# Layer 0 of a two-layer backbone: context tiles first, and their expert rows beside the latent tiles' attention

## The reference, cut to what matters

```
tokens: 256 context (2 tiles of 128) and 512 latent (4 tiles of 128), D = 1024, two layers, float32
for each layer:
    h  = modulated RMSNorm(x);  p = h @ w_in                 # 3104 columns
    y  = concat(GLA scan, 2-D neighbourhood attention ("nat"),
                differential attention with axial rotary ("diff"))
    x += gate * (y @ w_out)
    h2 = modulated RMSNorm(x)
    q  = h2 @ wq;  16 best of 128 x 128 product keys in each of 8 heads  -> 128 experts a token
    x += gate * sum over the 128 of  softmax_weight * gelu(h2 . U[expert]) * V[expert]
# context tokens read context tokens only; the last layer updates latent tokens only
out = RMSNorm(x)                                             # latent tokens
```

## Time and profile before

| | us |
|---|---|
| median of 3 executions | 4746.25 |
| lowest, highest | 4745.8, 4751.58 |
| span of the profiled execution | 4741.8 |

### The profile page before, as it was taken

One profiled execution on the slowest core, in us unless ns is written; L12 is line 12 of the kernel. 1 busy time (PEld: TensorE's weight loads), 2 busy tenths in 40 slices (PEclk: granted clock), 3 DMA queues, 4 the chain that ended last, 5 costly groups with the idle time before them and its releaser, 6 DMA issues. The chain is left out here.

```text
span 4741.8 us, 35603 instructions
## 1 busy us (share of the span) xinstructions
PE 2298.1 (48%) x11329; PEld 1110.8 (23%) x11329; DVE 2751.2 (58%) x6329; ACT 543.2 (11%) x1141; POOL 2607.1 (55%) x2676
## 2 busy tenths in 40 slices
PE   7995778815025034052067286688904205115025
PEld 3433655401001010010015253365601001001001
DVE  2117756983873963954944800575895493683840
ACT  1005652100000000000000000354100000000000
POOL 1101300577777767767766663140377777777775
PEclk9997999958558567576568698799957658657556
DMA  6840002799999999999999998002499999999998
GB/s 226 269 159 18 20 2 105 290 409 409 409 409 409 409 405 405 409 400 409 409 397 403 404 403 323 28 21 76 176 391 409 410 409 409 409 405 406 410 408 338
DMA packets 451030, 1495.96 MB, mean 315 GB/s; under 512 B 59506, under 2 KB 91974, under 8 KB 444190
## 3 DMA queue, kind: packets, MB, share of 16 engines
q0 software_dynamic: 368640, 1342.34, 71.4%
q1 hardware_dynamic: 46056, 76.70, 4.7%
q10 hardware_dynamic: 36150, 74.65, 4.6%
HBM read 1477.38 MB, written 16.14 MB: 315 GB/s over the span
## 5 line engine op out<-in xcount | busy, mean ns | idle before, releaser
L1612 POOL DMA_INDIRECT experts_U<-in_peer_u_dram,experts_expert x768 | 729.3, 950 | 695.5 <-PE experts_acc L1831 425.4
L2158 DVE CUSTOM_DVE_ANT_0 experts_V<-experts_V,experts_acc 128x1024 f32<-128x1024 f32 x512 | 622.2, 1221 | 584.4 <-DMA experts_V<-in_peer_u_dram,experts_expert 565.1
L2158 DVE CUSTOM_DVE_ANT_0 experts_U<-experts_U,experts_acc 128x1024 f32<-128x1024 f32 x768 | 930.5, 1220 | 52.0 <-DMA experts_U<-in_peer_u_dram,experts_expert 24.0
L1619 POOL DMA_INDIRECT experts_V<-in_peer_v_dram,experts_turned x640 | 608.6, 951 | 266.5 <-issue 179.3
L1619 POOL DMA_INDIRECT experts_U<-in_peer_v_dram,experts_turned x640 | 608.3, 951 | 229.2 <-issue 172.1
L1974 PE MATMUL experts_pair<-small,experts_w 128*128 128x128 f32 x10 | 4.7, 475 | 1437.7 <-DVE experts_w L2117 1437.7
L1988 PE MATMUL experts_acc<-experts_U,experts_lent 128*32 128x512 f32 x2560 | 443.5, 826 | 346.3 <-DMA experts_U<-in_peer_v_dram,experts_turned 346.3
L1988 PE MATMUL experts_acc<-experts_V,experts_lent 128*32 128x512 f32 x2560 | 432.8, 808 | 327.0 <-DMA experts_V<-in_peer_v_dram,experts_turned 327.0
L1612 POOL DMA_INDIRECT experts_V<-in_peer_u_dram,experts_expert x512 | 485.7, 949 | 174.7 <-issue 106.8
L1974 PEld LDWEIGHTS experts_pair<-small,experts_w 128*128 128x128 f32 x10 | 1.8, 182 | 1440.2 <-DVE experts_w L2117 1440.2
L430 PE MATMUL proj_acc<-W,HT 128*128 128x512 f32 (+2 forms) x832 | 327.3, 548 | 3.9 <-DMA W<-in_w_in_dram 2.5
(11 more groups left out here) (286 smaller groups left out, 3534.6 us busy)
## 6 DMA issues: line engine op xcount, KB each, us to landing
proj_ada<-in_ada_w_dram ACTq DMA_DIRECT2D x40, 1024.0 KB, 5.8
W<-in_w_in_dram SPq DMA_DIRECT2D x9, 2048.0 KB, 11.7
experts_U<-in_peer_u_dram,experts_expert POOLq DMA_INDIRECT x768, 14.2
experts_QT<-in_w_in_dram ACTq DMA_DIRECT2D x12, 960.0 KB, 19.4
experts_V<-in_peer_v_dram,experts_turned POOLq DMA_INDIRECT x640, 12.7
experts_U<-in_peer_v_dram,experts_turned POOLq DMA_INDIRECT x640, 12.7
PR<-in_ada_w_dram SPq DMA_DIRECT2D x8, 1024.0 KB, 17.0
experts_U<-in_w_out_dram SPq DMA_DIRECT2D x4, 2048.0 KB, 11.7
```

What stands on the lines that cost most here:

```text
L1612: pool.indirect_dma_start(into, None, u_rows, bass.IndirectOffsetOnAxis(ap=s.expert[:, j % 2, k:k + 1], axis=0)).then_inc(done, 16)
L1619: pool.indirect_dma_start(into, None, v_rows, bass.IndirectOffsetOnAxis(ap=s.turned[:, j % 2, e:e + 1], axis=0)).then_inc(done, 16)
L2158: nc.vector.tensor_tensor_reduce(out=rows, in0=rows, in1=h_bank(), scale=1.0, scalar=0.0, op0=ALU.mult, op1=ALU.add, accum_out=s.dots[:, j ...
```

## The change

Layer 0's attention now runs for the two context tiles only (`near`), and a new function, `experts_first`, does everything after it. It writes the row work of all six tiles as one stream for each engine: a generator that says before each piece which row it belongs to. `Advance.upto(n)` issues the pieces of rows below n. The stream is issued in five stretches:

- `early_head`: output projection, norm, queries and experts of the context tiles; rows 0 to 63
- `attention` "nat" of the latent tiles in a `Window` of rows 64 to 171: after each of 22 steps (6 preparations and 16 units) every engine issues the stream up to `at(i)`
- `attention` "diff" of the latent tiles in the same manner: rows 172 to 287, 22 steps
- `late_head`, head of the latent tiles: rows 288 to 399, 13 steps (5 for tiles, 8 for query heads)
- the main stretch: rows 400 to 1535

Tiles go in the order 0 to 5, 256 rows each, so tile 0 is rows 0 to 255 and tile 1 rows 256 to 511. Rows below 512 use 8 buffers, later ones 16. The context tiles' dots read h from SBUF (`Y`), the latent ones from PSUM as before. In the windows the scores have one PSUM buffer (`S_BUFS`), and queries, keys and values are read back from DRAM: `gla_scores` stores them there (`mix`, 6 DMAs, 7.1 MB), since the projection's SBUF is given up. The rotary operations move from "nat" to `gla_gates` in both layers. Five tiles (AHEAD) instead of four are projected for layer 1, in 65 units, 6 beside tile 4's V rows, 36 beside tile 5's U rows and 23 beside its V rows; the fifth of them, tile 4, is normalised among tile 5's dots. Layer 1 projects one tile, tile 5, with all its columns, and loads five.

```
-HIDDEN = 4
+AHEAD = 5
...
                 if not first:
-                    for t in range(t1, NT):
-                        act.dma_start(PR[:, t], m.pr[(t - t1) * P:(t - t1 + 1) * P]).then_inc(kept, 16)
-                    act.wait_ge(kept, 16 * HIDDEN)
+                    for t in range(AHEAD):
+                        act.dma_start(PR[:, t], m.pr[t * P:(t + 1) * P]).then_inc(kept, 16)
+                    act.wait_ge(kept, 16 * AHEAD)
...
-            neighbourhood(nc, m, l, PR, Y)
-            if stop == "nat":
-                return
-            differential(nc, m, l, PR, Y)
+            near = list(range(CT)) if l == 0 else list(range(CT, NT))
+            attention(nc, m, l, PR, Y, "nat", near, gated=True)
+            attention(nc, m, l, PR, Y, "diff", near)
...
-        experts(nc, m, l, t0, Y, out)
+        if l == 0:
+            experts_first(nc, m, Y)
+        else:
+            experts(nc, m, l, t0, Y, out)
...
+        rope = Y[:, 0, 0:LT * P].rearrange("p (t c) -> p t c", c=P)
+        r1, r2 = Y[:, 1, 0:512], Y[:, 2, 0:512]
+        rotary, turned = st.sem("rotary"), st.sem("turned")
...
+                if l == 0:
+                    for t in range(NT):
+                        sp.dma_start(m.mix[t * P:(t + 1) * P], PR[:, t, NQ:PROJ]).then_inc(spilled, 16)
+                    sp.wait_ge(spilled, 16 * NT)
...
+    def upto(self, n):
+        while self.place is not None and self.place < n:
+            self.place = next(self.steps, None)
...
+    def at(self, i):
+        return self.first + (self.last - self.first) * (i + 1) // self.steps
+
+    def pool(self):
+        self.stream.pool.upto(self.last + RING)
...
-    first_wide = wide.index(1)
-    with Stage(nc, f"{kind}{l}") as st:
...
+    first_wide = wide.index(1) if any(wide) else 0
+    own_rows = window is not None
+    S_BUFS = 1 if own_rows else 2
...
+        F = st.ps("F", [P, 4 + 2 * S_BUFS, 512])
...
+                if own_rows and not diff:
+                    sp.dma_start(rows[:], m.mix[:, 0:768].rearrange("(t p) c -> p t c", p=P)).then_inc(vals_in, 16)
+                if own_rows and diff:
+                    for t in range(NT):
+                        if t:
+                            sp.wait_ge(prep, t)
+                        sp.dma_start(raw[:], m.mix[t * P:(t + 1) * P, DQ - NQ:DQ - NQ + 1024]).then_inc(raw_in, 16)
+                    sp.dma_start(vals[:], m.mix[:, DV - NQ:DV - NQ + 512].rearrange("(t p) c -> p t c", p=P)).then_inc(vals_in, 16)
...
+                    if window is not None:
+                        window.pe(t)
...
+                    if window is not None:
+                        window.pe(NK_T + u)
...
+                    if window is not None:
+                        window.dve(NK_T + u)
...
+    SMALL_RING = CT * ROWS
+    HEAD_END, NAT_END, DIFF_END, LATE_END = 64, 172, 288, 400
...
+            if n < SMALL_RING:
+                return s.U[:, n % RING], ug[n % RING], 16 * (n // RING + 1)
+            turn, p = (n - SMALL_RING) // PLACES, (n - SMALL_RING) % PLACES
...
+                yield ROWS * j + SLOTS
+                pe.wait_ge(weights, j + 1)
+                pe.wait_ge(turned, j + 1)
...
+                for g in range(GROUPS):
+                    steps = LATE_STEP_AT if j == 1 else STEP_AT
+                    if 0 < j < T - 1 and g in steps:
+                        yield ROWS * j + SLOTS + GROUP * g
+                        key_scores(nc, pe, s, sems, 4 * (j + 1) + steps.index(g), s.QT[:, j + 1 - CT])
+                    yield ROWS * j + SLOTS + GROUP * g + GROUP - 1
...
+                    weighted_sum(j, g)
...
+                    if k == 0 and j >= CT:
+                        dve.wait_ge(held_h, j - CT + 1)
+                    nc.vector.tensor_tensor_reduce(out=rows, in0=rows, in1=s.h_bank if j >= CT else Y[:, j],
+                                                   scale=1.0, scalar=0.0, op0=ALU.mult, op1=ALU.add,
+                                                   accum_out=s.dots[:, j % 2, k:k + 1]).then_inc(dots, 1)
+                    if k in (OUT_AT, OUT_AT + 2):
+                        next(adding, None)
+                    elif k == TURNED_AT[j]:
+                        dve.wait_ge(etr, j + 1)
+                        nc.vector.tensor_copy(s.turned[:, j % 2], tr[:, 0:P]).then_inc(turned, 1)
+                    elif j == 0:
+                        next(s.finding, None)
...
+                    for x in range(2):
+                        nc.vector.scalar_tensor_tensor(out=s.next_sc[x], in0=s.next_sc[x], scalar=1.0, in1=s.next_g,
+                                                       op0=ALU.add, op1=ALU.mult).then_inc(next_coef, 1)
+                    for i in range(3):
+                        next_average(i)
...
+                        if i == 2:
+                            next_average(3)
+                        next_norm(i)
+            for _ in add_out(T - 1):
+                pass
...
+        stream.pool, stream.pe = Advance(row_steps(nc.gpsimd)), Advance(product_steps(nc.tensor))
+        stream.act, stream.dve = Advance(scalar_steps(nc.scalar)), Advance(dot_steps(nc.vector))
+        early_head(nc, m, Y, s, sems, stream, HEAD_END, acc, link, spare, gain, stat, sub_rows, zeroed, gates)
+        attention(nc, m, l, None, Y, "nat", LAT, window=Window(stream, HEAD_END, NAT_END))
+        attention(nc, m, l, None, Y, "diff", LAT, window=Window(stream, NAT_END, DIFF_END))
+        s.V = st.sb("V", [P, RING, D])
+        late_HT, s.QT = st.sb("HT", [P, KD, LT * P]), st.sb("QT", [P, LT, PH, P])
+        late_head(nc, m, Y, s, Window(stream, DIFF_END, LATE_END), link, late_HT, spare, gain, stat, late_gates)
...
+            def _(pool):
+                pool.wait_ge(prods, 2 * T)
+                stream.pool.upto(end + RING)
...
+                evacuate("h", 1)
+                for _ in range(40):
+                    next(s.finding)
+                stream.dve.upto(end)
...
+                for i in range(T + 1):
+                    if i < T:
+                        norm_heads(i)
+                        evacuate("y", i)
+                        residual(i, 0)
+                        residual(i, 1)
+                        dve.wait_ge(squared, i + 1)
+                        nc.vector.tensor_scalar(stat[:, 1, i:i + 1], stat[:, 0, i:i + 1], 1.0 / D, EPS, ALU.mult, ALU.add).then_inc(mean, 1)
+                    if i:
+                        evacuate("h", i - 1)
+                    if i < T:
+                        dve.wait_ge(root, i + 1)
+                        link(nc.vector.reciprocal(stat[:, 1, i:i + 1], stat[:, 2, i:i + 1]))
+                        link(nc.vector.scalar_tensor_tensor(out=Y[:, t0 + i], in0=m.X[:, t0 + i], scalar=stat[:, 1, i:i + 1], in1=sc,
+                                                            op0=ALU.mult, op1=ALU.mult))
+                        nc.vector.tensor_tensor(Y[:, t0 + i], Y[:, t0 + i], sh, ALU.add).then_inc(hs, 1)
+                    window.dve(i)
+                for h in range(PH):
+                    window.dve(T + 1 + h)
...
-    tiles = list(range(NT - HIDDEN, NT)) + list(range(CT, NT - HIDDEN)) + list(range(t0, CT))
+    tiles = list(range(t0, NT))
...
```

More of the change, by code:

```diff
@@ L393, in project @@
     WR, BANKS, AR = PROJ_RING, 3, 2
-    t1 = NT - HIDDEN if last else NT
-    EARLY = min(t1 - 1, BANKS)
+    tiles = list(range(AHEAD, NT)) if last else list(range(NT))
+    EARLY = min(len(tiles) - 1, BANKS)
     TABLES_AT = [[], [], [0, 1], [2, 3], [4, 5], [6], [7]]
@@ L410, in project @@
             table_in, table_out, windowed = (st.sem(x) for x in ("tablein", "tableout", "windowed"))
-        chunks = [x for x in PROJ_CHUNKS if x[2] or not last or t1 > CT]
-        work = [(c, t) for c in range(len(chunks)) for t in range(t1) if chunks[c][2] or not last or t >= CT]
+        chunks = PROJ_CHUNKS
+        work = [(c, t) for c in range(len(chunks)) for t in tiles]
         kept = st.sem("kept")
@@ L436, in early @@
                     product(pe, i - 1)
[L438 removed]
+            norm_modulate(nc, m, l, m.a["norm1_g"][l], 0, tiles[0], NT, HT, st, block, ht, scratch, after=early, ready=first)
             def window_table(sp, n):
@@ L940, in _, with __init__, spread, pe @@
                 evacuate(len(tiles) - 1)
-def neighbourhood(nc, m, l, PR, Y):
-    attention(nc, m, l, PR, Y, "nat")
-def differential(nc, m, l, PR, Y):
-    attention(nc, m, l, PR, Y, "diff")
-def attention(nc, m, l, PR, Y, kind):
+class Advance:
+    def __init__(self, steps):
+        self.steps = steps
+        self.place = next(steps)
+    def upto(self, n):
+        while self.place is not None and self.place < n:
+            self.place = next(self.steps, None)
+class Window:
+    def __init__(self, stream, first, last):
+        self.stream, self.first, self.last = stream, first, last
+    def spread(self, steps):
+        self.steps = steps
+    def at(self, i):
+        return self.first + (self.last - self.first) * (i + 1) // self.steps
```

(41 more changed lines are left out.)

1062 lines of the change are left out of this document (819 added, 243 removed).

## The result

The changed kernel took 4983.89 us in the median of 4 executions (4982.18 to 4990.04), against 4748.91 for the kernel before beside it: a ratio of 1.050, interval 1.0485 to 1.0515, slower by 235 us. The profiled execution's span is 4988.0 us, 246.2 more than before. The forecast was 4888.

What follows compares the result with a forecast made beforehand. Stages bound by PE and DVE alternate with stages bound by DMA. 4746.25 us, plus 144 from "nat" to row 512, less 2 elsewhere, gave 4888; own range 4810 to 4970, whole range 4640 to 5010.

Steps and rivals of the forecast that it cites:

- Context attention and `early_head`: Layer 0's context attention alone, 65 us, then `early_head` with rows 0 to 63 and retrieval on DVE, 205 us.
- "nat" window: Latent "nat" attention beside rows 64 to 171: 186 us for 108 rows, V groups at 7.0 us each.
- "diff" window: Latent "diff" attention beside rows 172 to 287: 246 us; units 10.5 us beside V rows, 13.1 beside U rows.
- `late_head`: Latent tiles' head beside rows 288 to 399: 255 us, PE and DVE alternating at 34.2 us a step.
- rival 2: Context U rows: each context dot holds up a gather by 0.60 us; +55 us, 4943 us; chance 0.06.
- Eight buffers as the limit of V rows: Rows below 512: only two V groups under way, 7.0 us a group; rows 400 to 511 take 182 us.
- rival 4: V rows below 512: eight buffers suffice at 5.1 us a group; -107 us, 4781 us; chance 0.10.
- Rotary operations: Gates' stage of both layers: they slow DVE where both read SBUF, +5 us (0 to 20).
- The fifth tile: Main stretch: 13 more projection units beside DMA-bound rows, hidden but for norm and stores, +8 us (0 to 40).
- Rival 1: Start of "nat" to row 512: windows hide everything and DMA sets the pace; -124 us, 4620 us; chance 0.22.
- Rival 3: Late window: PE falls to half clock, +66 us for turns and products, +30 for queries; 4984 us; chance 0.10.

Runs made afterwards that it cites:

- second experiment: Changed kernel with POOL stopping at each window's last row, and likewise in `early_head`, instead of running 8 rows ahead: 5297.83 us, ratio 1.0385 to the kernel before.
- fourth experiment: Changed kernel with late-head DVE dots moved after evacuating the next tile's turned rows, beside PE's output products: 5276.41 us, ratio 1.0328 to the kernel before.
- first experiment: Changed kernel with 16 buffers from row 408 instead of from row 512: 5278.66 us, ratio 1.0344 to the kernel before.

## Why the prediction was right, and where its terms were off

The direction, the mechanism and the range (4640 to 5010) held; the size was 96 us short, beyond the forecast's own range (4810 to 4970). By its own steps:

1. Context attention and `early_head` (270) were right: 271.6. DVE paced rows 0 to 63, with dots and retrieval in one order. But the price of a dot was read off a pair that followed DMA's pace, 1.27 us apart. Where rows lie ready, dots of the kernel before start every 1.14 us, as in this pair, so DVE does have some room beside U rows (1.14 of 1.29 us):

```profile
870.86 1.21 DVE L2158 CUSTOM_DVE_ANT_0 experts_U<-experts_U,experts_acc 128x1024 f32<-128x1024 f32 x1
871.99 1.22 DVE L2158 CUSTOM_DVE_ANT_0 experts_U<-experts_U,experts_acc 128x1024 f32<-128x1024 f32 x1
```

For 64 dots the sum is so 8 us too long; the stage end, 9.7 us, made up for it.
2. "nat" window: V groups came at 6.4 us in the mean (sums from 927.5 to 991.8, ten periods), under the 7.0 assumed. The term was short by the stage end: 11 us, where a stage end without gathers under way takes 1.5 (second experiment).
3. The four stage ends are the largest mechanism left out. Prefetching rows across a stage's end does not bridge it: the end waits until they have landed. It is some 38 us in all, where the sum had 1 for one barrier and the others within its terms of loads and turnover. Stopping early cost about as much (second experiment).
4. "diff" window: units beside V rows 10.9 us against 10.5, beside U rows 14.3 against 13.1, the unit at the turn from V to U rows 19.0, and a stage end of 7.0.
5. `late_head`: the alternation of PE and DVE was right, 34.9 us a step in the mean (33.8 to 36.0) against 34.2, and the fourth experiment took it out. Three things were mis-sized. DVE's first operation on the heads stands behind four rows of 512 KB that are queued after `w_out`, so the first product came after 24 us, not 13 (10.5 and 2.5 for turns). The last 62 dots took 89.7 us (1446.4 to 1536.1), not 78, at POOL's pace: this is rival 2's wait. And the stage end took 10.6. `wq`, 4.2 MB beside 75 gathers (358 GB/s from 1436 to 1553), wasn't in the sum either, but no wait of the changed kernel ends with it; in the fourth experiment PE waited 6.5 us for it.
6. Eight buffers as the limit of V rows: right, shown by 49 us less with sixteen. That refutes rival 4.
7. Rotary operations: 26 us for 5. They cost what the DVE operations beside them are held up, 39.86 us busy instead of 26.85 for the same 58, in layer 1.
8. The fifth tile was free on the chip of the first kind: rows 1280 to 1535, beside which all units but six stand, took 391.0 us instead of 391.5. The rest of the -4.5 lies in rows 512 to 1279.

Rival 1 (all is hidden) fell: no window over 300 GB/s. It was right that much is hidden, 173 us in the attention windows. But rows 0 to 511, from the first gather to row 512, took 1761.8 - 685.7 = 1076 us instead of 661.6. Those 414 us, less the 185 by which the first gather comes earlier after the start of "nat", are the 230.

Rival 2's wait is real. The prediction gave it little chance by a row that it misread. The gather of 0.96 us at 1445.61 did not run beside another operation with two SBUF inputs, but for 0.14 us; then DVE was at a reduction with one:

```profile
1443.27 1.23 DVE L1380 TENSOR_TENSOR experts_hot<-experts_partf,small 128x1024 f32<-128x1024 f32 x1
1444.53 1.22 DVE L1385 TENSOR_TENSOR experts_hot<-experts_hot,experts_idxf 128x1024 f32<-128x1024 f32 x1
1445.78 1.22 DVE L1388 TENSOR_REDUCE experts_sel<-experts_hot 128x64 f32<-128x1024 f32 x1
```

The Trainium skill (SBUF — State Buffer, "SBUF: two separate sides") says that a DVE instruction with two SBUF inputs and a GpSimd instruction that reads SBUF exclude each other for their whole length. The 1.98 us gathers fit it: 0.94 and most of a dot. But the wait doesn't fall on each gather, and 0.065 us a row is what it cost where it was measured alone. In the changed kernel it plainly set the pace in the last 62 dots of the late window, some 12 us of the rival's 55. Elsewhere DVE waited for U rows 5.3 us in `early_head` after the first, 3.9 in the "nat" window and not at all in "diff", so it can have cost little more there.

Rival 3 (half clock) gives the measured time, 4984, by accident: the late products took 15.5 to 16.8 us where the full clock takes 14, the granted clock was 0.72, and beside the queries (1446 to 1500) it was 0.96.

## What to carry to other kernels

Work laid beside other work in one fixed order per engine is paced by the slowest wait of each step, so price a window by each engine's own chain, not by the sum of idle times. A stage end with gathers under way costs their landing (7 to 11 us here), and stopping them early only moves the cost; whether fewer ends would give it back was not tried. And before moving a stage beside a stream bound by DMA, compare what the stage takes alone (here 150 us of attention and 118 of the head) with what the stream loses in pace beside it (2.10 us instead of 1.29 in each of 512 rows).

## What was not expected of the hardware

The same kernel takes 4745 us on one chip and 5105 on another, and 0.14 us in each of 2560 rows accounts for it; what makes the chips differ was not tried. On the second, plain loads beside the gathers suffer more than these. In the first 170 us of layer 0's last tile ACT issued two loads of 960 KB of the units' weights in the first experiment, where the changed kernel, whose code is the same there, issued six on the first kind. And the time of one and the same stretch of interleaved work differs between executions by 15 us (1220.3 to 1235.9).
